# Two decay products, an earlier first operand, and moved steps in a one-core decoder layer

## The reference

```python
x = x + 0.5 * swiglu_ffn(x, ffn1_norm, ...)        # rms_norm with a gain, gate and up 1024 -> 2816, down
h = rms_norm(x, mix_norm);  P = h @ w_in
y_gdn  = gated_deltanet(...)     # 4 heads x 128, chunks; decay = exp(gc_i - gc_j), gc = cumsum of g
y_moba = moba_attention(...)     # 4 heads x 64, causal, 2 blocks of 256
y_mem  = memory_attention(...)   # 4 heads x 64, 256 memory tokens
x = x + concat(y_gdn, y_moba, y_mem) @ w_out
x = x + 0.5 * swiglu_ffn(x, ffn2_norm, ...)
```

## Time and profile before

| | us |
|---|---|
| median of 3 runs | 994.4 (994.15 to 994.59) |
| the profiled execution | 994.35 |
| its span | 992.5 |
| PE busy | 987.5 (99% of the span) |
| DVE, POOL, ACT busy | 685.7, 509.7, 444.7 |

### The profile page before, as it was taken

The page is one execution under the profiler, slowest core; times in us unless marked ns, Lnnn a source line. Parts: engine busy times, 40 slices in busy tenths (PEclk is TensorE's granted clock), DMA queues, the critical chain, the costliest instruction groups (busy, mean ns, idle before and its releaser), DMA issues.

```text
span 992.5 us, 16521 instructions
## 1 busy us (share of the span) xinstructions
PE 987.5 (99%) x6833; PEld 872.2 (88%) x6833; DVE 685.7 (69%) x1092; ACT 444.7 (45%) x655; POOL 509.7 (51%) x297
## 2 busy tenths in 40 slices
PE   9999999999999999999999999999999999999998
PEld 7888999999999988788877888888999999999997
DVE  6894976676666497863547764789986676666745
ACT  8642444344443472534456764634343334433341
POOL 0355775676656433543252301645975666756741
PEclk9999999999999999999999999999999999999999
DMA  8432322332123312321221001322132333123312
GB/s 312 154 130 79 128 86 86 128 128 97 74 86 127 114 57 86 127 86 43 85 87 44 3 2 44 127 85 86 50 122 85 128 128 118 53 86 127 128 43 85
DMA packets 15914, 95.33 MB, mean 96 GB/s; under 512 B 2016, under 2 KB 2400, under 8 KB 5600
## 3 DMA queue, kind: packets, MB, share of 16 engines
q1 hardware_dynamic: 15696, 94.23, 26.4%
q10 hardware_dynamic: 144, 0.05, 0.0%
HBM read 92.17 MB, written 2.10 MB: 95 GB/s over the span
## 4 chain that ended last, share of the span: by engine, by line
PE 96%; DVE 3%; POOL 1%; issue 0%; ACT 0%; DVEq 0%; POOLq 0%
PE bank L2016 50%; PE bank L2142 35%; PE bank L2456 1%; PE bank L2542 1%; PE bank L2460 1%; PE bank L2482 1%; PE bank L2570 1%; PE bank L2559 1%; PE bank L2504 1%; PE bank L2194 1%; POOL wlo L517 0%; PE bank L2526 0%; DVE t_ffn_sum L1339 0%; PE bank L2606 0%; PE bank L2516 0%; PE bank L2628 0%
## 5 line engine op out<-in xcount | busy, mean ns | idle before, releaser
L2142 PE MATMUL bank<-t_ffn_hi,whi 128*128 128x256 f32 x952 | 269.4, 283 | 0.0
L2142 PE MATMUL bank<-t_ffn_hi,wlo 128*128 128x256 f32 x952 | 269.4, 283 | 0.0
L2142 PE MATMUL bank<-t_ffn_lo,whi 128*128 128x256 f32 x952 | 269.4, 283 | 0.0
L534 POOL TENSOR_TENSOR wlo<-sums,whi 128x512 fp32r<-128x512 f32 x136 | 184.7, 1380 | 131.8 <-ACT whi L739 131.7
L517 POOL TENSOR_TENSOR wlo<-raw,whi 128x1024 fp32r<-128x1024 f32 (+1 forms) x36 | 124.6, 3478 | 166.2 <-ACT whi L614 151.3
L534 POOL TENSOR_TENSOR wlo<-raw,whi 128x512 fp32r<-128x512 f32 x102 | 168.4, 1665 | 41.0 <-ACT whi L739 41.0
L2142 PEld LDWEIGHTS bank<-t_ffn_hi,whi 128*128 128x128 f32 x952 | 182.7, 192 | 0.7
L2142 PEld LDWEIGHTS bank<-t_ffn_lo,whi 128*128 128x128 f32 x952 | 182.7, 192 | 0.7
L2142 PEld LDWEIGHTS bank<-t_ffn_hi,wlo 128*128 128x128 f32 x952 | 182.7, 192 | 0.0
L2016 PE MATMUL bank<-ahi,whi 128*128 128x512 f32 x396 | 156.5, 395 | 0.4 <-POOL wlo L517 0.4
L2016 PE MATMUL bank<-ahi,wlo 128*128 128x512 f32 x396 | 154.4, 390 | 0.0
(11 more groups left out here) (339 smaller groups left out, 1405.1 us busy)
## 6 DMA issues: line engine op xcount, KB each, us to landing
raw<-fast_in SPq DMA_DIRECT2D x34, 1024.0 KB, 4.9
raw<-stream SPq DMA_DIRECT2D x26, 1024.0 KB, 4.9
raw_down<-fast_in SPq DMA_DIRECT2D x19, 1024.0 KB, 7.0
raw<-stream SPq DMA_DIRECT2D x7, 512.0 KB, 7.9
out<-x SPq DMA_DIRECT2D x7, 256.0 KB, 2.0
x<-x_in SPq DMA_DIRECT2D x3, 512.0 KB, 8.7
memx<-mem_in SPq DMA_DIRECT2D x2, 512.0 KB, 11.1
raw_gate<-stream SPq DMA_DIRECT2D x1, 1024.0 KB, 5.0
```

Source lines behind the costliest of these rows:

```text
L534: nc.gpsimd.tensor_tensor(in_ring(wlo, ring_at, n), whole[:, PIECE * at:PIECE * (at + 1)], in_ring(whi, ring_at, n).bitcast(F32), ALU.subt ...
L2142: ins = E.matmul(psum[bank][:, HALF * h:HALF * (h + 1)], a, b[:, k, :], start=start and k == 0 and m == 0, stop=k == K2 - 1 and m == 2, sk ...
```

## The change

- **Start.** The gains of FFN 1 now stand in the 8 columns ahead of x, in one tile `xg`, and arrive with the first piece of x. `small` is brought by SP, behind all five pieces, and no longer by ACT's queue. DVE, as its first step, makes the high part of k tile 0 of x; ACT goes on from k tile 1. `warm` is a quarter as wide, and PE runs 10 products on it. `first_pair` goes term by term for k tiles 0, 1 and 2.
- **Decay.** `columns` now keeps the parts of gc beside the norms' columns (at column 64), so that the second filling of `blocks` holds both. The four products of `prep_decay` for chunk 2, and the four for chunk 3, become one product each (`late_decays`), placed together where those of chunk 2 stood. In chunk 2 the banks of the two products of keys and queries are swapped.
- **Moves in the mixer.** DVE: the clearing of a part of `xt` goes behind `mk_scale(0)` and `mq_scale(0)`; the last evacuation of the input projection (`evacuate(25)`) and `prep_decay(2)` go ahead; the row maxima of block attention go behind `prep_scores(2)`. PE and ACT are reordered to match.
- **Move in FFN 2.** DVE adds output tile 3 ahead of the sums of weights. In FFN 1 the order stays.

```diff
@@ -185,7 +186,7 @@
+        warm, _, _ = place("warm", [P, P], F32R, at=mid)
         msum, _, _ = place("msum", [P, M], at=at_at + 3 * M * 4)
...
@@ -252,7 +253,7 @@
-            return small[:, c:c + 1]
+            return small[:, c:c + 1] if c >= 0 else xg[:, KD + c:KD + c + 1]
...
         R_BANKS = [7, 5]
-        PREP_BANKS = [(4, 5, 6), (4, 5, 6), (0, 4, 6), (1, 5, 0)]
...
-                sp.dma_start(x[:, k0:k1, :], x_in[:, k0:k1, :]).then_inc(x_sem[i], 16)
+                x0, x1 = KD + k0 * T if k0 else 0, KD + k1 * T
+                sp.dma_start(xg[:, x0:x1], x_in[:, x0:x1]).then_inc(x_sem[i], 16)
+            sp.dma_start(small[:], small_in).then_inc(small_sem, 16)
...
             A = nc.scalar
-            A.dma_start(small[:], small_in).then_inc(small_sem, 16)
-
...
                     part_hi(u, c0, c1, w0_in[n], 16, piece_hi)
-                for d in range(PIECES[i], PIECES[i + 1]):
+                for d in range(max(PIECES[i], 1), PIECES[i + 1]):
+                    if d == 1:
+                        act.wait_ge(a_hi, 1)
...
                 x_square(0, d)
+            act.wait_ge(small_sem, 16)
             A.activation(gain_qk[:, 0:1], col(S_MQ), ACT.Copy, scale=col(S_MK)).then_inc(gain_ready, 1)
...
             level_copy(0, 6)
+            mem_copy(5)
+            prep_decay(2)
             mem_weights(7, 0)
             mem_weights(7, 1)
-            mem_copy(5)
-            prep_decay(2)
             prep_decay(3)
-            weights(0, 0)
             mem_copy(6)
             prep_keys(2)
+            weights(0, 0)
             mem_copy(7)
             prep_keys(3)
...
+            dve.wait_ge(x_sem[0], 16)
+            V.tensor_scalar(x_hi[0][:, 0, :], x[:, 0, :], col(S_G1), None, ALU.mult).then_inc(a_hi, 1)
...
                     part_lo(u, c0, c1, piece_hi, n + 1, piece_lo)
-                if i == 0:
-                    dve.wait_ge(small_sem, 16)
                 for d in range(PIECES[i], PIECES[i + 1]):
                     x_low(0, S_G1, d)
+            dve.wait_ge(small_sem, 16)
...
                 ffn_add(before, 2)
+                if f == 1:
+                    ffn_add(before, 3)
                 first_sums(f, 0, 1)
-                ffn_add(before, 3)
+                if f == 0:
+                    ffn_add(before, 3)
                 other_sums(f, 0, 1)
...
-            V.memset(xt[half[1], 0:2, :, half[0]], 0.0).then_inc(corner_zero, 1)
             mk_scale(0)
             mq_scale(0)
+            V.memset(xt[half[1], 0:2, :, half[0]], 0.0).then_inc(corner_zero, 1)
             level_update(0, 4)
...
+            evacuate(25, z[:, 3, :])
             mem_max(6, 0)
             mem_max(6, 1)
             level_update(0, 5)
             mem_out(4)
             mem_scale(5, 0)
             mem_scale(5, 1)
-            evacuate(25, z[:, 3, :])
+            prep_decay(2)
             mem_scale(6, 0)
             mem_max(7, 0)
             mem_max(7, 1)
             link(V.tensor_tensor(inv0[:, 0:16], rq, rq, ALU.mult))
             mem_scale(6, 1)
-            prep_decay(2)
             prep_decay(3)
+            level_update(0, 6)
+            mem_out(5)
+            prep(2)
+            prep_scores(2)
             row_max(0, 0)
-            mem_out(5)
             row_max(0, 1)
-            prep(2)
-            level_update(0, 6)
-            prep_scores(2)
             prep_query(2)
             mem_scale(7, 0)
...
-                pe.wait_ge(piece_hi, 1)
-                pe.wait_ge(a_hi, 1)
-                for (w, act_), (done, count) in zip(((whi, ahi), (wlo, ahi), (whi, alo)),
-                                                    ((a_hi, 1), (piece_lo, 1), (a_lo, 1))):
-                    pe.wait_ge(done, count)
-                    for bank in range(4):
-                        E.matmul(psum[bank][:], wslice(w, 0, 0, bank * P, P, PAIR), act_[:, 0, :],
-                                 start=w is whi and act_ is ahi, stop=False)
-                for k in range(1, KD):
+                for k in range(3):
+                    low = (piece_lo, k + 1) if k < 2 else (w_lo, 1)
+                    pe.wait_ge(*((piece_hi, k + 1) if k < 2 else (w_hi, 1)))
+                    for (w, act_), (done, count) in zip(((whi, ahi), (wlo, ahi), (whi, alo)),
+                                                        ((a_hi, k + 1), low, (a_lo, k + 1))):
+                        pe.wait_ge(done, count)
+                        for bank in range(4):
+                            E.matmul(psum[bank][:], wslice(w, 0, k, bank * P, P, PAIR), act_[:, k, :],
+                                     start=k == 0 and w is whi and act_ is ahi, stop=False)
+                for k in range(3, KD):
                     pe.wait_ge(a_hi, k + 1)
...
-                    for _ in range(11):
-                        E.matmul(psum[4][:], warm[:, 0:P], warm[:], start=True, stop=True)
+                    for _ in range(10):
+                        E.matmul(heads(4), warm[:], warm[:].unsqueeze(1).broadcast_to([P, H, P]), start=True, stop=True)
...
-            def prep_decay(c):
-
-                if c == 2:
-                    pe.wait_ge(mk_ready, 5)
-                else:
-                    pe.wait_ge(p_evac, 26)
-                for h in range(H):
-                    i = E.matmul(heads(PREP_BANKS[c][0])[:, h, :], gcol(G_G, h, c).broadcast_to([P, P]), upper,
-                                 start=True, stop=True)
-                    if c == 2 and h == 0:
-                        i.then_inc(w_used, 1)
-                i.then_inc(prep_ps[0], 1)
+            def late_decays():
+
+                pe.wait_ge(mk_ready, 5)
+                E.matmul(psum[PREP_BANKS[2][0]][:], picks[:, 2:3].broadcast_to([P, P]), blocks,
+                         start=True, stop=True).then_inc(w_used, 1)
+                pe.wait_ge(p_evac, 26)
+                E.matmul(psum[PREP_BANKS[3][0]][:], picks[:, 3:4].broadcast_to([P, P]), blocks,
+                         start=True, stop=True).then_inc(prep_ps[0], 2)
 
             def prep(c):
 
...
-                    pe.wait_ge(y_sb, 3 * LAST)
+                    pe.wait_ge(x_upd, n_x(0, LAST))
                 elif c == 3:
...
                 qb = PREP_BANKS[c][2]
-                if c == 3:
+                if c == 2:
+                    pe.wait_ge(y_sb, 3 * LAST)
+                elif c == 3:
...
             mem_out(4)
-            prep_decay(2)
+            late_decays()
             level_first(0, 6)
             mem_scores(7)
             mem_turn(5)
-            prep_decay(3)
             prep(2)
+            level_second(0, 6)
+            mem_out(5)
+            prep_scores(2)
+            mem_turn(6)
+            prep_turn(2)
             scores(0)
-            mem_out(5)
-            level_second(0, 6)
-            mem_turn(6)
-            prep_scores(2)
             mem_out(6)
-            prep_turn(2)
...
     r = np.where(i < 64, i % 16, -64)[:, None]
-    c[:, C_BLK:C_BLK + 4] = r // NC_ == n
-    c[:, C_BLK + 4:C_BLK + 8] = (r >= 0) & (r % 8 // 2 == n)
-    c[:, C_PICK:C_PICK + 4] = (r >= 0) & (r % NC_ == n)
+    c[:, C_BLK:C_BLK + 4] = ((r >= 0) & (r % 8 // 2 == n)) | (decay // NC_ == n)
+    c[:, C_PICK:C_PICK + 4] = (decay >= 0) & (decay % NC_ == n)
```

More of the change, by code:

```diff
@@ L62 @@
 C_BLK = C_SEL + 2
-C_PICK = C_BLK + 8
+C_PICK = C_BLK + 4
 C_N = C_PICK + 12
-S_G1, S_GM, S_G2, S_GMEM = 0, KD, 2 * KD, 3 * KD
-S_CONV = 4 * KD
+S_G1, S_GM, S_G2, S_GMEM = -KD, 0, KD, 2 * KD
+S_CONV = 3 * KD
 S_OG = S_CONV + 12 * 4
@@ L99, in sem @@
             return ctx.enter_context(nc.semaphore(name))
-        x, _, _ = place("x", [P, KD, T])
+        xg, _, _ = place("xg", [P, KD + KD * T])
+        x = xg[:, KD:KD + KD * T].rearrange("p (k t) -> p k t", k=KD)
         ahi, a_hi0, _ = place("ahi", [P, KD, T], F32R)
@@ L187, in build @@
         memsq, _, _ = place("memsq", [P, KD, M], at=cq_at)
-        warm, _, _ = place("warm", [P, T], F32R, at=mid)
+        warm, _, _ = place("warm", [P, P], F32R, at=mid)
         msum, _, _ = place("msum", [P, M], at=at_at + 3 * M * 4)
@@ L402, in build @@
         R_BANKS = [7, 5]
-        PREP_BANKS = [(4, 5, 6), (4, 5, 6), (0, 4, 6), (1, 5, 0)]
+        PREP_BANKS = [(4, 5, 6), (4, 5, 6), (0, 6, 4), (1, 5, 0)]
         CONV_BANKS, CK_BANK = (4, 5), 7
@@ L2880, in constants @@
     r = np.where(i < 64, i % 16, -64)[:, None]
+    decay = np.where((i >= 64) & (i < 96), i % 16, -64)[:, None]
     keys = (i // 16 % 2 == 1)[:, None]
     n = np.arange(4)[None, :]
-    c[:, C_BLK:C_BLK + 4] = r // NC_ == n
-    c[:, C_BLK + 4:C_BLK + 8] = (r >= 0) & (r % 8 // 2 == n)
-    c[:, C_PICK:C_PICK + 4] = (r >= 0) & (r % NC_ == n)
+    c[:, C_BLK:C_BLK + 4] = ((r >= 0) & (r % 8 // 2 == n)) | (decay // NC_ == n)
+    c[:, C_PICK:C_PICK + 4] = (decay >= 0) & (decay % NC_ == n)
     pairs = (r // 8 == n // 2) & (r % 2 == n % 2)
@@ L2945 @@
     small = np.concatenate(
-        [per_partition(a[n][0]) for n in ("ffn1_norm", "mix_norm", "ffn2_norm", "mem_norm")]
```

(4 more changed lines are left out.)

6 lines of the change are left out of this document (2 added, 4 removed).

## The result

The changed kernel is slower: 997.19 us (median of 10 runs, 996.93 to 998.81) against 994.39 (10 runs, 994.03 to 994.59), ratio 1.0032, interval 1.0022 to 1.0042. The forecast was 992.8, range 991.7 to 993.8. The profiled execution took 997.81 us with a span of 996.0. In short: the edits work, but one of them moves the weights by 32 bytes in the SBUF, and that slows products that nobody edited.

What follows compares the result with a forecast made beforehand. PE, busy 987.5 of 992.5 us, was taken to bound the kernel. 994.35 - 0.2 (start) - 0.41 (525 us) - 1.0 (decay) - 0 (FFN 2) = 992.74, so a median of 992.8 us, range 991.7 to 993.8.

Steps and rivals of the forecast that it cites:

- Behind it everything is bound by PE until the mixer, and moves with it: Stretch from the start to the mixer: PE alone sets the time, so the start's 0.2 us gain passes on.
- The start, 0.2 forecast: First products on PE: x scaled sooner by DVE starts them some 0.3 us earlier, worth 0.2, between 0 and 0.45.
- a sign that it is wrong: Start: the prediction calls itself wrong if the stretch up to k tile 3 is longer than before.
- The rule on misaligned rows: x's DMA: rows off a 256-byte boundary cost an extra transaction, eating about 0.1 us of the start's 0.2.
- 525 us, 0.41 forecast: Mixer: PE's spreading product no longer waits for DVE's `mk` behind the clearing of `xt`; 0.41 us saved.
- Decay products, 0.66 forecast for two: Mixer, 535 to 540 us: two products take 0.66 us where two groups took 1.98; 1.32 removed.
- The new wait of 0.3 ahead of chunk 3's transposes: Mixer: DVE's last `at` gains 1.43 us, PE wants 1.73; the 0.3 wait leaves 1.0 of 1.32.
- FFN 2, 0.5 moved 20 us down: The 0.5 us wait at 697 us goes but returns on POOL near 717 us, so the gain is 0.
- All of it arrives: Rival, 30%: clock rises with the start (0.4), no new wait at chunk 3 (1.32), POOL ends sooner (0.5): 991.8 us.
- The clock's rival: Start, 8%: fewer idle products leave PE idle 0.5 us, the clock rises later, real products run at 1.2 GHz: 995.0 us.

Runs made afterwards that it cites:

- b_shift32: The kernel before with only a 32-byte tile placed behind x, no instruction changed: 999.19 us for 994.40.
- a_front32: The changed kernel with all its edits, but xg begun 32 bytes lower, so x and every tile behind it stand where they stood before: 992.26 us for 994.29.
- start_only: The kernel before with only the start's edits, all tiles at the addresses of before: 994.13 us for 994.29.
- best5: The kernel before with all the change's edits, x's rows 256-byte aligned in HBM, five of each FFN's seven t tiles 192 bytes behind the weights' remainder: 979.94 us for 994.30.

## Why the prediction was wrong

**The step that failed** is the sentence in the part on the start, "Behind it everything is bound by PE until the mixer, and moves with it", with the premise at the head of the prediction that time can come only from an earlier start, from products taken off, or from waits. Both take the speed of PE's products as given by their shape. The edit `place("xg", [P, KD + KD * T])` was costed for its DMA and its scaling, never for the 32 bytes by which it moves the weights. That is +4.8 us by b_shift32 (999.19 less 994.40), as the count of spacings gives. With a_front32's -2.0 the sum is +2.8, which is what was measured (997.19 less 994.39). No rival had this mechanism, so the range did not hold it.

**The start, 0.2 forecast.** At the old addresses k tile 3 came 0.58 sooner, more than forecast: 0.26 from the earlier first product (6.05 for 6.31), and most of the rest because the clock had risen before it (products 0.25 apart from 6.05 on). That was luck, since start_only rose late with the same start. In the changed kernel k tile 3 came 0.30 later, which the prediction had named as a sign that it is wrong: a wait for the third piece of x, which the prediction doesn't have, took what the start had won. The median of start_only is only 0.16 lower. The rule on misaligned rows, which I priced at 0.1 and at the first piece, would act on the third; ACT took that one up 1.3 us later than before (11.54 for 10.22), and how much of this is the rule's is not shown.

**525 us, 0.41 forecast:** 0.39 at the spreading product itself in a_front32, and 0.50 with the product behind it, since one that starts afresh also takes 0.34 to the next start where one in a row takes 0.23. **Decay products, 0.66 forecast for two:** 0.67, and the 1.32 us came off. The new wait of 0.3 ahead of chunk 3's transposes is absent: DVE's last `at` ended at 546.16, 2.5 us sooner than before and not 1.4, and PE came at 546.22, so 1.2 us were passed on for 1.0. **FFN 2, 0.5 moved 20 us down:** right. The lead grew from 2.43 to 2.94 at the last tile of `down` and was 2.43 again from 717.9 on, behind POOL. Another 0.2 us of lead grew in FFN 1 without an edit there, and no part of the sum accounts for it. All told, the profiled execution of a_front32 leads by 2.4 us where 1.6 were forecast, and the median gained 2.0.

**The rivals.** No rival had the addresses. *All of it arrives* had three pieces, and without the side effect two of them came true in the profile (the earlier clock, and no wait at chunk 3), while POOL held the third. The clock's rival, priced at 995.0, was right as a mechanism for some executions of start_only (995.7). It has no part in the changed kernel's profile, whose first real products run fast; two of that kernel's ten runs lie at 998.6 and 998.8, which stays open.

## What to carry to other kernels

A tile that grows by a few bytes moves every tile behind it, and on a kernel bound by TensorE that can be worth more than the edit: compare the mean spacing of untouched products in the two traces before any wait. Keep tile sizes ahead of the weights at multiples of 256 bytes, or pad them, and test the distance between stationary and moving operand as a tuning knob of its own: the best layout found here (best5) doesn't have all of them at distance 0. Where an edit costs time in stretches that it doesn't touch and PE doesn't wait there, look at the addresses.
